# Two gate projections taken out of the split-weight tiles and computed in float32 on four column groups

## What is computed

```
h = rmsnorm(x, norm_mix_g[l])
proj = h @ a_w_in[a]
qk, v, o, gates, q_mem = jnp.split(proj, [2 * A_WIDTH, 3 * A_WIDTH, 4 * A_WIDTH, 4 * A_WIDTH + 2 * A_HEADS], axis=-1)
gates = gates.astype(jnp.float32) + a_gate_b[a].astype(jnp.float32)
ig, fg = jnp.split(gates, 2, axis=-1)
...
h = rmsnorm_2(x, norm1_g[l])
proj = jnp.einsum('bsd,de->bse', h, w_in[l])
dq, dk, dv, fq, fk, fv, fg = jnp.split(proj, SPLITS, axis=-1)
...
log_f = jax.nn.log_sigmoid((fg + b_f[l]).astype(f32))
```

## Time and profile before

| | us |
|---|---|
| median of three runs | 1882.55 |
| lowest and highest run | 1876.22, 1882.86 |
| the profiled execution | 1878.44 |
| its span | 1876.7 |
| TensorE busy | 1843.1 (98%) |
| VectorE busy | 928.9 (49%) |
| ScalarE busy | 742.4 (40%) |
| GpSimd busy | 275.0 (15%) |

### The profile page before, as it was taken

The page is one execution under the profiler, slowest core; times in us unless marked ns, Lnnn a source line. Parts: engine busy times, 40 slices in busy tenths (PEclk is TensorE's granted clock), DMA queues, the critical chain, the costliest instruction groups (busy, mean ns, idle before and its releaser), DMA issues.

```text
span 1876.7 us, 21708 instructions
## 1 busy us (share of the span) xinstructions
PE 1843.1 (98%) x8914; PEld 1504.1 (80%) x8914; DVE 928.9 (49%) x1439; ACT 742.4 (40%) x1184; POOL 275.0 (15%) x241
## 2 busy tenths in 40 slices
PE   8999999999999999999999999999999999999998
PEld 7877678888888898667888888878876788888886
DVE  6667555542453435745543344456666433323334
ACT  5645344331333424654433133342557333212223
POOL 2000222220121100001221022112001122201210
PEclk9999999999999999999999999999999999999999
DMA  6122132222222323212232222231121222322221
GB/s 224 68 96 74 45 112 85 96 105 98 90 90 96 115 104 136 79 34 92 88 106 96 103 100 84 87 121 68 68 90 46 87 94 90 108 95 90 102 84 62
DMA packets 31666, 173.89 MB, mean 93 GB/s; under 512 B 3392, under 2 KB 5568, under 8 KB 13648
## 3 DMA queue, kind: packets, MB, share of 16 engines
q1 hardware_dynamic: 26320, 163.03, 24.5%
q10 hardware_dynamic: 5248, 9.47, 1.6%
HBM read 170.36 MB, written 2.13 MB: 92 GB/s over the span
## 4 chain that ended last, share of the span: by engine, by line
PE 89%; DVE 5%; ACT 3%; issue 1%; DMA 1%; POOL 0%; SPq 0%; ACTq 0%; DVEq 0%; POOLq 0%
PE ps L938 50%; PE ps L1182 18%; PE ps L882 7%; PE ps L957 6%; PE ps L1093 2%; PE ps L1048 2%; PE ps L1073 1%; DVE WL L1656 1%; PE ps L1132 1%; DMA raw<-in_wall 1%; PE ps L1113 1%; ACT PB L1409 1%; ACT WH L1255 1%; PE ps L862 0%; PE ps L871 0%
## 5 line engine op out<-in xcount | busy, mean ns | idle before, releaser
L938 PE MATMUL ps<-hH,WH 128*128 128x512 f32 x1472 | 580.9, 395 | 3.8 <-DVE WL L1656 1.3
L938 PE MATMUL ps<-hH,WL 128*128 128x512 f32 x1472 | 573.7, 390 | 0.0
L938 PE MATMUL ps<-hL,WH 128*128 128x512 f32 x1472 | 573.5, 390 | 0.0
L1656 DVE TENSOR_TENSOR WL<-raw,WH 128x1024 fp32r<-128x1024 f32 (+2 forms) x312 | 382.6, 1265 | 382.9 <-ACT WH L1255 382.8
L1255 ACT ACTIVATE WH<-raw 128x1024 fp32r<-128x1024 f32 (+2 forms) x312 | 303.4, 1020 | 279.6 <-PE ps L1182 228.7
L938 PEld LDWEIGHTS ps<-hH,WH 128*128 128x128 f32 x1472 | 276.4, 188 | 68.5 <-issue 9.5
L938 PEld LDWEIGHTS ps<-hL,WH 128*128 128x128 f32 x1472 | 276.5, 188 | 58.8 <-issue 2.6
L938 PEld LDWEIGHTS ps<-hH,WL 128*128 128x128 f32 x1472 | 276.4, 188 | 58.0
L1182 PE MATMUL ps<-fH,WL 128*128 128x512 f32 x528 | 205.6, 389 | 0.0
L1182 PE MATMUL ps<-fH,WH 128*128 128x512 f32 x528 | 205.6, 389 | 0.0
L1182 PE MATMUL ps<-fL,WH 128*128 128x512 f32 x528 | 205.6, 389 | 0.0
(11 more groups left out here) (336 smaller groups left out, 1999.4 us busy)
## 6 DMA issues: line engine op xcount, KB each, us to landing
raw<-in_wall SPq DMA_DIRECT2D x140, 1024.0 KB, 4.6
raw<-in_wall SPq DMA_DIRECT2D x12, 768.0 KB, 4.0
bias<-in_bias ACTq DMA_DIRECT2D x12, 256.0 KB, 3.2
X<-in_xt SPq DMA_DIRECT2D x8, 256.0 KB, 10.0
CB<-rows ACTq DMA_DIRECT2D x8, 256.0 KB, 3.4
out_y<-X SPq DMA_DIRECT2D x3, 512.0 KB, 3.0
raw<-in_wall SPq DMA_DIRECT2D x4, 256.0 KB, 5.6
mrA<-in_memt ACTq DMA_DIRECT2D x4, 256.0 KB, 6.3
```

Of the source, the lines that this page charges most:

```text
L938: mm = e.matmul(ps[b][:, 0:N], ww[:, k, c:c + 128], x[:, k, 0:N], start=(k == 0 and i == 0), stop=(k == 7 and i == 2))
L1656: e.tensor_tensor(WL[n % NCV][:, c], raw[n % NRAW][:, c], WH[n % NCV][:, c].bitcast(F32), ALU.subtract).then_inc(*mark("wl", n, x))
```

## The change

The eight gate columns of both blocks are no longer part of a tile of split weights. A new input `gatew` brings them (`graw`, 128x8x8), with a matrix `gsum` that adds four groups of 32 partitions. VectorE multiplies them by the norm's gain into `gw` (32 columns for each k, of which eight are not zero; GpSimd clears the rest once). TensorE multiplies X itself by them in float32: k = 0 and 4 into output partitions 0 to 31, 1 and 5 into 32 to 63, and so on, so that eight products stand in four column groups of one bank. One eviction multiplies by `Rsb`, and a product with `gsum` adds the four groups. In the first block input and forget gates are now two such products. In the third block one values tile pair stands where the gate tile and the second query pair stood, and `x_final` is put earlier.

```diff
-    u += [("a_w_in", 0, 0, 8, 3072, 128), ("a_w_in", 0, 0, 8, 3080, 256)]
+    u += [("a_w_in", 0, 0, 8, 3080, 256)]
...
-    u += [("w_in_2", 0, 0, 8, 0, 256), ("w_in_2", 0, 0, 8, 2952, 128)]
-    u += [("w_in_2", 0, 0, 8, 256 * j, 256) for j in (1, 2, 3, 4, 5, 6, 8, 10, 7, 9, 11)]
+    u += [("w_in_2", 0, 0, 8, 256 * j, 256) for j in (0, 4, 1, 2, 3, 5, 6, 8, 10, 7, 9, 11)]
...
+    put("gate_weights", "A")
     for k in range(8):
         put("scaled", "mix0", k, None)
...
     rstd("mix0", 60)
-    fm(1, "mix0", "gate", "gate")
+    put("gate_products", "A")
+    waiting.append(("gate",))
     fm(1, "mix0", "qmA", "R")
...
+    put("gate_products", "C")
+    waiting.append(("fg",))
     fm(1, "n1", "dq", "rope")
-    fm(1, "n1", "fgate", "fg")
+    tm(1, "n1", "dv", "v")
     fm(1, "n1", "dq", "rope", m0=2)
-    fm(2, "n1", "dk", "rope")
-    for j in range(2):
-        for i, _ in enumerate(g_tm(1, "n1", "dv", "v", u0=j)):
-            put("x_final", 4 * j + 2 * i)
-            put("x_final", 4 * j + 2 * i + 1)
+    for i, _ in enumerate(g_fm(2, "n1", "dk", "rope")):
+        put("x_final", i)
+    for i, _ in enumerate(g_tm(1, "n1", "dv", "v", u0=1)):
+        put("x_final", 4 + 2 * i)
+        put("x_final", 5 + 2 * i)
...
+                elif what == "gate_products":
+
+                    b, before = bank("gates" + a[0], ("gate",) if a[0] == "A" else ("fgG",))
+                    if before:
+                        w.wait_ge(*at(*before))
+                    w.wait_ge(*at("gwD", a[0]))
+                    w.wait_ge(*at("gw0"))
+                    for k in range(8):
+                        if a[0] == "A":
+                            w.wait_ge(s_x[k] if ev.sems else None, 16)
+                        else:
+                            w.wait_ge(*at("xf", 1, 1, k))
+                        r = slice(32 * (k % 4), 32 * (k % 4) + 32)
+                        mm = e.matmul(ps[b][r, :], gw[:, k, :], X[:, k, :], start=(k < 4), stop=(k >= 4))
+                    mm.then_inc(*mark("glin", a[0]))
+
...
-                    e.matmul(ps[b][0:4, :], ident[0:8, 4:8], O[0:8, 0, :], start=True, stop=True).then_inc(
+                    e.matmul(ps[b][0:4, :], gsum[:, 4:8], O[:, 0, :], start=True, stop=True).then_inc(
                         *mark("gates", "f"))
+                    b, before = bank("gi", ("gateD", "i"))
+                    if before:
+                        w.wait_ge(*at(*before))
+                    e.matmul(ps[b][0:4, :], gsum[:, 0:4], O[:, 0, :], start=True, stop=True).then_inc(
+                        *mark("gates", "i"))
...
-                    e.matmul(ps[b][0:8, :], ident[96:128, 120:128], Gf[96:128, :], start=True, stop=True).then_inc(
-                        *mark("fgates"))
+                    e.matmul(ps[b][0:8, :], gsum[:, :], Gf[:, :], start=True, stop=True).then_inc(*mark("fgates"))
...
-                    e.tensor_scalar(gt, O[0:4, 0, :], col("gi", p=slice(0, 4)), None, ALU.add).then_inc(
+                    w.wait_ge(*at("gates", "i"))
+                    e.tensor_scalar(gt, ps[BANK["gi"]][0:4, :], col("gi", p=slice(0, 4)), None, ALU.add).then_inc(
...
+            e.dma_start(gsum[:, :], gatew[:, 64:72]).then_inc(s_gw, 16)
+            e.dma_start(graw[:, :, :], gatew[:, 0:64].rearrange("p (k c) -> p k c", k=8)).then_inc(s_gw, 16)
             load(1)
```

More of the change, by code:

```diff
@@ L579, with program @@
     affine_select = dma_start = then_inc = wait_ge = _
-def program(nc, wall, xt, memt, colsd, biasd, consts, rope, out):
+def program(nc, wall, xt, memt, colsd, biasd, consts, rope, gatew, out):
     ctx = ExitStack()
@@ L705, in program @@
         CB = [place(f"CB{i}", [128, 512]) for i in range(2)]
+        gw = place("gw", [128, 8, 32], offset=227840)
+        gsum = place("gsum", [128, 8], offset=228864)
+        graw = place("graw", [128, 8, 8], offset=228896)
         m_rows = nc.dram_tensor("m_rows", (8, 512), F32, kind="Internal").ap()
@@ L817, in last_part @@
             return 1 if n else 3
-        drains = {"mkcp": "mkv", "mvcp": "mkv", "gate": "gate", "R": "linR", "conv_in": "cvin", "o": "linR",
-                  "v": "vev", "g": "fg", "u": "fz", "fg": "fgG", "rope": "ropeU"}
+        drains = {"mkcp": "mkv", "mvcp": "mkv", "R": "linR", "conv_in": "cvin", "o": "linR",
+                  "v": "vev", "g": "fg", "u": "fz", "rope": "ropeU"}
         BANK, FREED = {}, {}
@@ L1255, in scalar @@
                     e.activation(WH[n % NCV][:, c], raw[n % NRAW][:, c], ACT.Copy).then_inc(*mark("wh", n, x))
+                elif what == "gate_weights" and a[0] == "C":
+                    w.wait_ge(*at("gwD", "A"))
+                    e.dma_start(graw[:, :, :], gatew[:, 72:136].rearrange("p (k c) -> p k c", k=8)).then_inc(s_gw, 16)
                 elif what == "sqrt_table":
@@ L1622, in diagonal, with times_R @@
                         *mark("diag", what, i))
-            def times_R(dst, src, scale=None, rows=slice(0, 128)):
+            def times_R(dst, src, scale=None):
                 if scale is None:
-                    return e.tensor_tensor(dst, src, Rsb[rows, :], ALU.mult)
-                return e.scalar_tensor_tensor(out=dst, in0=src, scalar=scale, in1=Rsb[rows, :], op0=ALU.mult,
+                    return e.tensor_tensor(dst, src, Rsb[:, :], ALU.mult)
+                return e.scalar_tensor_tensor(out=dst, in0=src, scalar=scale, in1=Rsb[:, :], op0=ALU.mult,
                                               op1=ALU.mult)
@@ L1715, in vector @@
                     diagonal("join", small[:, 32:36], ("rcol", "n1"))
+                elif what == "gate_weights":
+                    if a[0] == "A":
+                        w.wait_ge(s_cols if ev.sems else None, 16)
+                        w.wait_ge(s_gw if ev.sems else None, 32)
+                        w.wait_ge(*at("gw0"))
+                    else:
+                        w.wait_ge(s_gw if ev.sems else None, 48)
+                        w.wait_ge(*at("glin", "A"))
+                    g = (col("mix0", 0, 8) if a[0] == "A" else gg[:, :]).rearrange("p (k c) -> p k c", c=1)
+                    e.tensor_tensor(gw[:, :, 0:8], graw[:, :, :], g.broadcast_to([128, 8, 8]), ALU.mult).then_inc(
+                        *mark("gwD", a[0]))
                 elif what == "gate":
-                    name, m = a
-                    w.wait_ge(*at("lin", name, m))
+                    w.wait_ge(*at("glin", "A"))
                     w.wait_ge(*at("Rsb", "mix0"))
-                    times_R(O[0:8, 0, :], ps[BANK[(name, m)]][0:8, :], rows=slice(0, 8)).then_inc(
-                        *mark("gate", name, m))
+                    times_R(O[:, 0, :], ps[BANK["gatesA"]][:, :]).then_inc(*mark("gate"))
                 elif what == "gates_later":
@@ L2096, in gpsimd @@
                     e.memset(diag[:, :], 0.0).then_inc(*mark("zero"))
+                    e.memset(gw[:, :, :], 0.0).then_inc(*mark("gw0"))
                     e.memset(small[:, 60:61], 1e-6).then_inc(*mark("eps", 0))
@@ L2379 @@
     consts, rope = shape_constants()
+    gates = [w.reshape(8, 128, 8).transpose(1, 0, 2).reshape(128, 64)
+             for w in (z["a_w_in"][0][:, 3072:3080], z["w_in_2"][0][:, 3072:3080])]
+    group = np.tile(np.concatenate([np.eye(8, dtype=np.float32), np.zeros((24, 8), np.float32)]), (4, 1))
     arrays = {
@@ L2383 @@
         "cols": cols, "bias": bias, "consts": consts, "rope": rope,
+        "gatew": np.concatenate([gates[0], group, gates[1]], 1),
     }
```

13 lines of the change are left out of this document (7 added, 6 removed).

## The result

The changed kernel took 1874.62 us (median), the kernel before 1879.57 in the runs beside it: a ratio of 0.9975 with a 95% interval of 0.9966 to 0.9984, or 4.7 us (3.0 to 6.4) less. The forecast was 4.4 us, and 1878.1 us as a time; of the 3.5 us between this and 1874.62, 3.0 are the kernel before, whose first three executions had a median of 1882.55. The profiled execution took 1874.93 us with a span of 1873.2, against 1878.44 and 1876.7: 3.5 us less.

A forecast was written before the change was run, and what follows sets the result against it. TensorE (98% busy) was taken as the bound, except VectorE and ScalarE from 54.9 to 104.4 us. First block 0.7 plus third block 3.7 gave 4.4 us off the 1882.55 median: 1878.1 us, 8-in-10 range 1869.5 to 1883.5.

The forecast's parts named there:

- Products 1.9 us: First block: the eight gate products run side by side on four column groups and take 1.9 us.
- The first rival: Column groups run serially, products 6.9 us; third block's last products 2.2 us later; total 1884.2, chance 0.08.
- Sums at 36.0: First block: sums of squares start at 36.0 instead of 34.91, behind a transfer landing 1.1 us later.
- Values 0.7 earlier: First block: the memory heads' values start 0.7 us earlier, not the 5.5 us of the removed gate tile.
- S+49.1: First block: second softmax reduced 49.1 us after the sums start (S), against S+50.5 before.
- 69.5 - 1.8: First block: time in us from the sums to the values, 69.5 less a gain of 1.8.
- the last wait: First block: the values still wait for the transposed probabilities PTA, by 2 us or more.
- The wait at q2: First block: TensorE waits 2 to 4 us ahead of tile q2 for its weights WL.
- From 104 us on nothing of it differs: Behind the first block's values start nothing changes, so what is gained by then stays.
- Third block 3.7: Third block: 5.5 (gate tile) + 1.3 (hL) + 1.65 (diag) - 4.8 (products) = 3.7 us gained.
- next late is nothing that I find: Third block: with the diag wait gone no new wait appears; diag comes about 2 us before its turn.
- The total: Whole kernel: 0.7 + 3.7 = 4.4 us gained, giving 1878.1 us.

The follow-up runs named there:

- order_only: Kernel before, with only the third block's first values unit and x_final moved, gate tile kept; third block 86.95 us against 87.35, one execution.
- c_only: Kernel before with only the third block of the changed kernel, first block keeping its gate tile; ratio 0.9985 (0.9974 to 0.9996).
- a_only: Changed kernel with its third block put back, so only the first block is changed; ratio 0.9994 (0.9984 to 1.0004).
- groups: Changed kernel with the eight products on two column groups in the first block and one in the third; third block 87.14 us, one execution.
- spin_A: Changed kernel plus 40 filler matmuls in TensorE's wait at 231 us; fillers took 8.9 us, TensorE 1.31 us later at 242, one execution.
- prod_in_late: fg_late with the third block's products inside the first dq tile, ahead of k=7; third block 80.53 us, one execution.
- fg_late: Changed kernel with the third block's forget gate steps one tile later each; third block 83.35 us against 84.95, one execution.
- ga_late: Changed kernel with the first block's gate sigmoid and logarithm behind both k tiles; total 1874.01 us, one execution.
- all_edits: Changed kernel with the edits of prod_in_late and ga_late plus 20 fillers at 231 us; 1864.46 us, ratio 0.9929 (0.9916 to 0.9941).

## Why the prediction came out as it did

- **Products 1.9 us**: right, 1.92. The rule of the Trainium skill that was weighed against it ("TensorE: Matmul & The Clock Gate", what overlaps and what doesn't: a weight load overlaps only where its row group differs; 2.4 us by it) isn't borne out: sixteen passes with their loads take just four passes' time of 0.43 and a start. The first rival was priced right for the third block (2.2, measured 2.19).
- **Sums at 36.0**: right, 35.97, with the landing 1.06 later. Across the kernels with the same transfers they start at 35.6 to 36.3, and without them they start at 34.67 (order_only), 34.91 and 35.70 (c_only): a landing scatters by about as much as the term, so the hit to 0.03 us is luck.
- **Values 0.7 earlier**: 0.55 in after, 0.89 in a_only. The reduction at S+49.2 was forecast at S+49.1, and the queue behind the gates' activations was named. From the sums to the values 69.5 - 1.8 was forecast and 67.90 measured, so 1.6 in place of 1.8. The size of the last wait was wrong: 0.72 for `PTA`, not 2 or more; in a_only, groups, spin_A, prod_in_late and fg_late it is 1.6 to 1.9. The wait at q2 (3.57) lies in the 2 to 4 forecast. What was left out is the half clock behind it, which took TensorE's lead in place of the last wait: from 80 to 85 and from 85 to 90 us the granted clock was 0.53 and 0.79 in after, 0.77 and 0.89 in a_only.
- **"From 104 us on nothing of it differs"**: this step failed for the profile of after (0.55 was gone by 1235) and held for a_only (0.61 left). What it missed is again the clock.
- **Third block 3.7**: measured 2.40. Gate tile, `hL`, `diag` and the products with their wait came as in the sum; what failed is "next late is nothing that I find". It was the eviction into `U`, 1.43 us. 2.40 + 1.43 = 3.83; fg_late, which takes away this wait alone, gives 4.00. The prediction followed VectorE's order for `diag` and did not follow ScalarE's queue one tile further. Also `diag` ended at 1265.4 with its turn at 1265.8, a margin of 0.4 us and not of 2.
- **The total**: 4.4 forecast, 4.7 (3.0 to 6.4) by the medians. The mechanisms account for 0.6 + 2.4 = 3.0 us, the low end, and it is luck that the two totals agree so closely. The lowest executions of the two kernels, 1876.22 and 1873.62, lie 2.6 us apart. That the profiled span shows 3.5 is the clock of the last matmuls, 1.3 us, which the prediction did not have, less what the clock took from the lead of the first block.

## What to carry to other kernels

Where an edit takes a wait away, follow each engine's queue one tile past it: what stood behind the removed work (here an eviction and a conversion behind two table loads on ScalarE, and an eviction behind the gates' chain on VectorE) may be next late. Put small independent work inside a tile, just ahead of the step that waits, so that two waits cover each other: this was worth 2.8 us, more than the whole edit of the third block as it was made (2.4). A float32 product with few output columns costs by passes of its column group, and four groups run at once.

## What the runs showed of the hardware that I had not expected

After a wait of TensorE the granted clock falls to half (1.2 GHz) in some executions and not in others, and when it comes back differs too. Behind the same wait of 2.24 us it was 0.66 in ga_late and 1.00 in all_edits (the two windows above). Windows of the second block, behind a wait of 2.2 us, first of before, then of order_only, which is the same program there:

```profile
819.00:821.00 2.00, 2.00 (x21) 1.33 (x16) 1.54 (x9) 2.00 (x9) 0.00 (x0) 1.00 0.00 0
```

```profile
819.00:821.00 2.00, 2.00 (x6) 0.61 (x8) 1.97 (x10) 1.50 (x5) 0.00 (x0) 0.50 0.04 8
```

In before the half clock ended at 817, in order_only between 821 and 823; its lag behind before grew there by 1.9 us, from 0.7 to 2.6. In ga_late it held from 810 to 819, and the lead on after fell there from 4.0 to 1.1 us:

```profile
815.00:820.00 5.00, 5.00 (x22) 2.30 (x19) 1.77 (x10) 4.83 (x17) 0.00 (x0) 0.53 0.01 3
```

Behind the wait at 231 the pitch of the matmuls fell from 0.43 to 0.23 us at 240.2 in before and at 240.5 in after, which cost after most of its lead: 0.56 us before the wait, 0.07 behind it. In the second block it lost another 0.26. At the end of the kernel before, a_only, groups and prod_in_late had the half clock, and after, c_only, order_only, fg_late, ga_late and spin_A not; the same stretch is 1.2 to 1.3 us longer with it. The first tile of c_only behind the sums is one more such place (1.6 us). So there are five places, of which each moves the span by up to 1.0 to 2.9 us in a way that no edit here explains. Together that is more than the change itself; a stretch has to be measured from its own start. That it is a matter of the execution, and not only of the kernel, is seen in before: 19 of its executions, taken beside a_only, have spans from 1874.3 to 1881.2 us, with a mean granted clock of 0.998 in the shortest and 0.991 to 0.992 in the four longest. The Trainium skill ("TensorE: Matmul & The Clock Gate", Part 1) says of a kernel's start that how many matmuls run at the lower level varies from run to run of one kernel; these rows show the same in mid-kernel. Fillers in the wait kept the clock at full where they were tried (231 us), which took this scatter away in that place.
